# Whole expert blocks in paired slot halves, and layer two's filter taps in row pairs, in a two-layer hybrid encoder

## What is computed

```python
for i in range(DEPTH):                                   # DEPTH = 2
    h = modulate(rms_norm(x, norm1_g[i]), sh1, sc1)
    proj = h @ w_in[i]                                   # 1024 x 6656
    y_hy = hyena_mixer(...)      # its filters: k = (sin-MLP(z) @ w4) * decay
    y_at = dilated_attention_mixer(q, k, v)
    x = x + g1 * ((sigmoid(gate_hy) * (y_hy @ w_br_h[i]) + sigmoid(gate_at) * (y_at @ w_br_a[i])) @ w_out[i])
    h = modulate(rms_norm(x, norm2_g[i]), sh2, sc2)
    x = x + g2 * grouped_moe(h, router_w, router_bias, moe_w1[i], moe_w3[i], moe_w2[i])
return rms_norm(x, final_g)
# grouped_moe: two experts a token;  y += gate_e * ((silu(t @ w1[e]) * (t @ w3[e])) @ w2[e])
```

## Time and profile before

| | us |
|---|---|
| median of 3 runs | 1050.93 (1049.51 to 1054.65) |
| the profiled execution | 1051.37 |
| its span | 1049.6 |
| PE busy | 1001.3 (95%) |
| DVE busy | 564.4 (54%) |
| ACT busy | 188.5 (18%) |
| POOL busy | 40.0 (4%) |
| read from memory | 329.47 MB |

### The profile page before, as it was taken

How to read it: one execution, slowest core, us unless ns; L and a number is a source line. 1 busy time by engine, 2 the same in 40 slices (tenths; PEclk the granted TensorE clock), 3 DMA queues, 4 the chain that set the end, 5 groups by cost and what they waited for, 6 DMA issues and landing times.

```text
span 1049.6 us, 18343 instructions
## 1 busy us (share of the span) xinstructions
PE 1001.3 (95%) x7711; PEld 603.9 (58%) x7711; DVE 564.4 (54%) x1192; ACT 188.5 (18%) x395; POOL 40.0 (4%) x82
## 2 busy tenths in 40 slices
PE   6999999999999999999999999999999999999784
PEld 3688667667785444443358866765878534444321
DVE  4578795868786223352235779672758622333112
ACT  4031001211233121011131110132123311110102
POOL 2100100010000000000010010001000000000000
PEclk9999999999999999999999999999999999999997
DMA  9998946297976999999999894627875599999991
GB/s 310 385 383 299 309 162 242 71 315 287 407 300 219 421 387 420 421 420 421 421 397 367 287 328 163 222 71 273 312 277 213 199 421 421 421 419 421 421 419 76
DMA packets 91851, 333.88 MB, mean 318 GB/s; under 512 B 5724, under 2 KB 6027, under 8 KB 66933
## 3 DMA queue, kind: packets, MB, share of 16 engines
q1 hardware_dynamic: 87937, 323.56, 79.4%
q0 software_dynamic: 2944, 7.12, 2.3%
q10 hardware_dynamic: 884, 1.97, 0.6%
HBM read 329.47 MB, written 1.05 MB: 315 GB/s over the span
## 4 chain that ended last, share of the span: by engine, by line
PE 83%; DVE 9%; DMA 3%; issue 2%; ACT 1%; SPq 1%; DVEq 0%; ACTq 0%
PE bank L822 80%; DMA ring<-in_moe_w_dram 2%; SPq L721 1%; PE bank L1335 1%; PE bank L1111 1%; DVE wide L2004 0%; DVE area L2000 0%; DVE wide L1796 0%; PE bank L1164 0%; DVE x L2220 0%; PE bank L885 0%; DVE area L2219 0%; DVE area L2196 0%; DVE wide L2005 0%; DVE area L2003 0%
## 5 line engine op out<-in xcount | busy, mean ns | idle before, releaser
L822 PE MATMUL bank<-ring,hT 128*32 128x512 f32 (+3 forms) x1808 | 280.2, 548 | 4.9 <-DMA ring<-in_moe_w_dram 2.1
L822 PE MATMUL bank<-hT,ring 128*32 128x256 f32 (+1 forms) x2112 | 213.5, 381 | 0.7 <-DVE hT L1820 0.7
L822 PEld LDWEIGHTS bank<-ring,hT 128*32 128x32 f32 (+2 forms) x1808 | 119.8, 133 | 137.8 <-issue 132.5
L822 PEld LDWEIGHTS bank<-hT,ring 128*32 128x32 f32 (+1 forms) x2112 | 158.6, 132 | 53.3 <-issue 6.1
L822 PE MATMUL bank<-ring,area 128*32 128x512 f32 (+1 forms) x744 | 119.4, 571 | 0.9 <-ACT area L1670 0.9
L822 PE MATMUL bank<-area 32*64 32x64 f32 (+5 forms) x648 | 89.1, 363 | 0.0
L1796 DVE SCALAR_TENSOR_TENSOR area<-ring,wide,area 128x512 f32<-128x512 f32 x114 | 85.3, 748 | 2.7
L2428 DVE TENSOR_TENSOR area<-bank,area 128x512 f32<-128x512 f32 x14 | 9.7, 692 | 128.9 <-PE bank L822 128.9
L822 PE MATMUL bank<-wide,hT 128*32 128x512 f32 (+1 forms) x376 | 76.8, 584 | 1.4 <-DMA ring<-in_moe_w_dram 1.4
L822 PEld LDWEIGHTS bank<-ring,area 128*32 128x32 f32 (+1 forms) x744 | 43.8, 121 | 55.2 <-issue 50.1
L822 PEld LDWEIGHTS bank<-area 32*64 32x64 f32 (+4 forms) x648 | 37.9, 145 | 45.6 <-issue 44.4
(11 more groups left out here) (302 smaller groups left out, 1082.1 us busy)
## 6 DMA issues: line engine op xcount, KB each, us to landing
ring<-in_moe_w_dram SPq DMA_DIRECT2D x136, 1024.0 KB, 15.2
ring<-in_w_ada_dram SPq DMA_DIRECT2D x24, 2048.0 KB, 14.5
ring<-in_w_in_dram SPq DMA_DIRECT2D x24, 2048.0 KB, 12.3
wide<-in_moe_w_dram SPq DMA_DIRECT2D x32, 1024.0 KB, 12.9
cst<-in_moe_w_dram SPq DMA_DIRECT2D x13, 1024.0 KB, 13.2
area<-in_moe_w_dram SPq DMA_DIRECT2D x11, 1024.0 KB, 13.7
ring<-in_w_out_dram SPq DMA_DIRECT2D x4, 2048.0 KB, 8.6
ring<-in_w_br_h_dram SPq DMA_DIRECT2D x4, 1536.0 KB, 6.7
```

What stands on the lines that cost most here:

```text
L822: return pe.matmul(dst, lhsT, rhs, start=start, stop=stop, skip_group_check=True)
```

## The change

It has two parts, in one kernel.

**Whole blocks.** `place_blocks` now looks, at the first half of a block of steps 1 to 5, among the oldest two free slots for one whose other half stands at most one place behind it or before it in the list. If there is one, the two halves of that expert's matrix go together into this pair, as one DMA of 2 MiB ([128, 4096], 16 KiB a partition instead of 8), which SP issues where the first half stood; it waits for the release of both slots, and both halves of the matrix are ready when all 2 MiB have landed. In layer one 20 blocks are loaded whole, in layer two 23; every other one is as before. What is behind moves to other slots and so waits for other releases.

**Taps in pairs.** The w4 pieces of b = 0 stay on rows 64 to 127, those of b = 1 now land on rows 0 to 63, and GpSimd copies layer two's rows of `fh` also to rows 0 to 63 (one DMA more, 64 x 257). The products are issued by turns from the upper and the lower rows, into banks 2 to 5. Step 3 does 4 of them, before `up(3, 1)`, with no wait for DVE between them; the other 4 are done in step 4, before `up(4, 1)`. DVE reads them there too, so in step 4 ahead of `butterfly`. `scatter` waits for DVE bank by bank.

```diff
@@ place_blocks
-                    u, old = free.pop(0)
-                    while (L, u) in LAST and b[0] > LAST[L, u]:
+                    if (L, b) in whole and half:
+                        continue
+                    free = [f for f in free if b[0] <= LAST.get((L, f[0]), STEPS)]
+                    near = [i for i in range(2) if free[i][0] < TABLE and free[i][0] ^ 1 in [f[0] for f in free[:i + 2]]]
+                    if half == 0 and b[0] in WHOLE_STEPS and near:
+                        u = free[near[0]][0] & ~1
+                        olds = [old for f, old in free if f in (u, u + 1)]
+                        free = [f for f in free if f[0] & ~1 != u]
+                        whole.add((L, b))
+                        for h in range(2):
+                            part = (L, kind, b, h)
+                            plan[part] = halves[u + h], u, landings[u] + 16, olds[:1] if olds[0] == olds[1] else olds
+                            free.append((u + h, part))
+                    else:
                         u, old = free.pop(0)
-                    plan[key] = halves[u], u, landings[u] + 16, [old]
-                    free.append((u, key))
+                        plan[key] = halves[u], u, landings[u] + 16, [old]
+                        free.append((u, key))
...
@@ taps_in, tap, tap_bank
-        def taps_in(L, s, spot):
-            return range(4 * spot, 4 * spot + 4) if L + 1 < DEPTH and s == TAPS_STEP else ()
+        def taps_in(L, s):
+            first = 4 * (s - TAPS_STEP)
+            return range(first, first + 4) if L + 1 < DEPTH and s in (TAPS_STEP, TAPS_STEP + 1) else ()
+
+        def tap(l, i):
+            return i % 2 * 4 + i // 2 if l else i
+
+        def tap_bank(l, i):
+            return bank[2 + i % 4] if l else filter_bank(l, i % 2)
...
@@ SP
+                    if (L, b) in whole:
+                        dst, part = pairs[u // 2], slice(0, 2 * rows)
...
@@ GpSimd
+                    pool.wait_ge(p_kt, 8)
+                    pool.dma_start(fh[0:FFN, :], fh[FFN:2 * FFN, :]).then_inc(s_taps, 16)
...
@@ taps, on PE
-                    if u >= 2:
-                        pe.wait_ge(v_kt, l * 12 + u - 1)
+                    if l == 0 and i >= 2:
+                        pe.wait_ge(v_kt, i - 1)
+                    elif l and i >= 4:
+                        pe.wait_ge(v_kt, l * 12 + i - 3)
...
-                    mm(dst, fh[l * FFN:(l + 1) * FFN, first:first + P], hw4(l, b, n), True, True).then_inc(p_kt, 1)
+                    mm(tap_bank(l, i)[:, 0:HW2], fh[tap_rows(l, b), first:first + P], hw4(l, b, n), True, True)\
+                        .then_inc(p_kt, 1)
...
@@ scatter
-                            if L + 1 < DEPTH and k == 2 and s + 1 in (TAPS_STEP, TAPS_STEP + 1):
-                                pe.wait_ge(v_kt, (L + 1) * 12 + 4 * (s + 2 - TAPS_STEP))
+                            if taps_in(L, s + 1):
+                                pe.wait_ge(v_kt, (L + 1) * 12 + 4 * (s + 1 - TAPS_STEP) + k + 1)
...
@@ DVE, step s
-                    for u in taps_in(L, s, 0):
-                        decayed(u, L + 1)
+                    for i in taps_in(L, s):
+                        decayed(i, L + 1)
                     if L + 1 < DEPTH and s == TAPS_STEP + 1:
                         butterfly(L + 1, 0)
```

More of the change, by code:

```diff
@@ L78 @@
 TABLE, TAIL, ROWS = EXTRA + 4, EXTRA + 5, EXTRA + 6
+WHOLE_STEPS = range(1, 6)
 LAST = {(0, EXTRA): 3, (0, EXTRA + 1): 3, (0, EXTRA + 2): 1, (0, EXTRA + 3): 1, (1, EXTRA + 2): 3, (1, EXTRA + 3): 3}
@@ L224, in trunk_kernel @@
         halves += [cst[:, C_IC:C_IC + 4 * W]]
+        pairs = ring + [wide[:, h * 8 * W:(h + 1) * 8 * W] for h in range(2)]
         Kr = hy[:, 0:2 * HY].rearrange("p (m c) -> p m c", m=2)
@@ L370, in trunk_kernel, with tap_rows @@
         fing = g1b
+        def tap_rows(l, b):
+            half = l - b if l else 0
+            return slice(half * FFN, (half + 1) * FFN)
         def hw4(l, b, n):
-            rows = slice(l * FFN, (l + 1) * FFN)
+            rows = tap_rows(l, b)
             if l == 0:
                 return taps0[rows, b * HY + n * HW2:b * HY + (n + 1) * HW2]
-            if (b, n) == (1, 1):
-                return hT[rows, 0:HW2 // P, P:SEQ]
-            return ((rates, vec_rows), (attended,))[b][n][rows, 0:HW2]
+            return ((rates, vec_rows), (attended, vec_rows))[b][n][rows, 0:HW2]
         bank = [ctx.enter_context(nc.psum_tensor(f"bank{i}", [P, 512], F32)) for i in range(8)]
@@ L552, in trunk_kernel @@
         plan = {}
+        whole = set()
         def place_blocks():
@@ L683, in _ @@
             for L, kind, b, half in loads:
+                if half and (L, b) in whole:
+                    continue
                 _, u, _, olds = plan[L, kind, b, half]
@@ L719, in _ @@
                     name, order = ("moe_w1", "moe_w3", "moe_w2")[m], "(p k) f -> p k f"
-                    part = slice(half * (NF if m == 2 else ND) // 2, (half + 1) * (NF if m == 2 else ND) // 2)
+                    rows = (NF if m == 2 else ND) // 2
+                    part = slice(half * rows, (half + 1) * rows)
+                    if (L, b) in whole:
+                        dst, part = pairs[u // 2], slice(0, 2 * rows)
                     sp.dma_start(dst.rearrange("p (k f) -> p k f", f=D if m == 2 else FE),
@@ L809, in _ @@
                             src = t["hf_w4"][1, :, b * HY + n * HW2:b * HY + (n + 1) * HW2]
-                            if (b, n) == (1, 1):
-                                src = src.rearrange("k (a f) -> k a f", f=P)
                             pool.dma_start(hw4(1, b, n), src).then_inc(s_taps, 16)
+                    pool.wait_ge(p_kt, 8)
+                    pool.dma_start(fh[0:FFN, :], fh[FFN:2 * FFN, :]).then_inc(s_taps, 16)
             pool.wait_ge(p_up, DEPTH * STEPS * 2)
@@ L1384, in next_filter @@
                         rates_to_all(L + 1)
-                    if taps_in(L, s, spot) or spectra_in(L, s, spot):
+                    here = taps_in(L, s) if spot == 0 else ()
+                    if here or spectra_in(L, s, spot):
                         pe.wait_ge(v_acc, (L * STEPS + s - 1 + spot) * 4)
-                    for u in taps_in(L, s, spot):
-                        taps(u, L + 1)
+                    for i in here:
+                        taps(i, L + 1)
                     for u in spectra_in(L, s, spot):
@@ L1854, in shift_and_scale, with decayed @@
                     dv.wait_ge(v_A1, l + 2)
-                def decayed(u, l):
+                def decayed(i, l):
+                    u = tap(l, i)
                     b, lt, n = u // (2 * NT), u // 2 % NT, u % 2
                     dv.wait_ge(a_dec, 8 * l + u + 1)
-                    dv.wait_ge(p_kt, l * 8 + u + 1)
+                    dv.wait_ge(p_kt, l * 8 + i + 1)
                     taps = decays[l][:, b, lt, n * HW2:(n + 1) * HW2]
-                    dv.tensor_tensor(taps, filter_bank(l, n)[:, 0:HW2], taps, ALU.mult).then_inc(v_kt, 1)
+                    dv.tensor_tensor(taps, tap_bank(l, i)[:, 0:HW2], taps, ALU.mult).then_inc(v_kt, 1)
                 def butterfly(l, half):
@@ L2433, in _ @@
                         rows_to_h().then_inc(v_hg, 1)
-                    for u in taps_in(L, s, 1):
-                        decayed(u, L + 1)
                     for h in range(2):
```

10 lines of the change are left out of this document (4 added, 6 removed).

## The result

| | kernel before | the change |
|---|---|---|
| first comparison: median, us | 1050.93 (1049.51 to 1054.65, 7 runs) | 1057.04 (1054.71 to 1060.52, 7 runs) |
| ratio | | 1.0049 [1.0029, 1.0070] |
| both once more, in a later comparison | 1052.71 | 1059.8, ratio 1.0076 [1.0051, 1.0101] |
| span of the profiled execution, us | 1049.6 | 1058.6 |

The account below looks back on a forecast made before the run. The prediction took the weight stream on SP's queue to bound both mixtures, with PE waiting on landings. Layer one's later `up(5, 1)` +3.8, slow clock +1.7, layer two -0.4 made +5.1 us: 1056.0 us, range 1050 to 1061.

Parts of the forecast that it names:

- The stream bounds the middle of layer one: Layer one, `up(5, 1)`: weights only 4.0 us ahead of PE, so anything PE saves earlier beyond that is waited away.
- Granularity: Layer one, first half of `up(5, 1)`: with whole blocks it needs MiB 78 instead of MiB 75.
- The slow clock behind the wait: Layer one, after PE idles 8 us before `up(5, 1)`: products run at about half clock, adding 1.7 us.
- The restart, 3.4 us: Layer one: first load waits for both halves of `up(0, 0)`, so the stream starts 3.4 us late.
- The gap at MiB 49: Layer one: new gap, whole w2 block (MiB 49 and 50) waits for slots freed by `down(2)`; about 1.0 us.
- The count itself: Landing times from queue start, 2.494 us a MiB, gaps, and 5.2 us for start and last landing; held within 0.1 us.
- Packet size, 0.09 us a block: Whole blocks with 16 KiB packets take 0.09 us less than two halves; 1.6 us for 18 blocks in layer one.
- The rival of slower packets: 16 KiB packets slower than two of 8 KiB, 5.1 us a block: 10.4 us with the clock, 1061.3 us; 15%.
- slices under 415 GB/s: Sign that the forecast is wrong: slices over 428 or under 415 GB/s.
- Taps, 1.3 us for four: Four tap products, paired side by side, take 1.3 us; 2.6 if the pairs don't overlap.
- The wait before `up(4, 1)`, 1.5 us: Layer one: PE comes at 449.3 us, MiB 62 of the whole w3 blocks at 450.8, so 1.5 us waited.
- Layer two, -0.4 us: Wait moves to `down(5)`, which needs MiB 84 instead of 81; then PE runs without a wait, ending 0.4 us earlier.

Follow-up runs that it names:

- the change again: The change run once more, unaltered, on the chip of the later kernels; ratio to the kernel before 1.0076 [1.0051, 1.0101].
- taps_only: The change's taps with every block loaded in halves as in the kernel before; 1054.45 us beside 1053.94, ratio 1.0016.
- one_block: The change's taps, only the three w3 blocks of layer one's step 5 whole, all others in halves; 1057.01 us beside 1053.14, ratio 1.0042.
- grain: The change, but with the three w3 blocks of layer one's step 5 loaded in halves; 1055.69 us, ratio 1.0018.
- same_rows: The change with the tap products in plain order, so only one of three neighbouring pairs has different rows; single run, 1056.88 us.
- restart: The change, but the w3 block of layer one's step 1, expert 1, where the queue starts again, loaded in halves; 1059.28 us, ratio 1.0070.
- whole_only: The change's whole blocks in both layers, with the taps as in the kernel before; 1060.43 us beside 1053.94, ratio 1.0069.
- keep_clock: The change with 16 dummy 128x256 products ahead of `up(5, 1)` in layer one, in the wait; 1058.81 us, ratio 1.0063.
- four_split: The change with the restart's block, MiB 25 and 26, MiB 49 and 50, and step 5's w3 of layer one in halves; 1053.1 us beside 1052.71, ratio 1.0005.
- l2_whole: The change's taps, layer one's blocks all in halves, layer two's 23 whole as in the change; 1053.34 us beside 1053.14, ratio 1.0007.

## Why the prediction was right, and where it wasn't

The total was right, +5.1 us predicted and 5.2 between the profiles counted from S (6.8 with the change again; 6.1 and 7.1 between medians), and so was its place. That `up(5, 1)` started within 0.1 us of the forecast was partly luck: two errors in the count cancel. Step by step:

- **The stream bounds the middle of layer one; what PE saves there is waited away.** Right. taps_only shows it by itself: 5.1 us earlier at `up(5, 1)`, 0.2 us at the end of the layer.
- **Granularity: `up(5, 1)` needs MiB 78 in place of 75.** Right, and the main term: one_block makes 4.3 us of it alone, grain takes 3.2 away.
- **The slow clock behind the wait, 1.7 us.** Right in kind; the size is 1.6, 1.6 (same_rows), 2.0, 2.2, 2.6, 2.7 and 2.7 us in the seven profiles that wait with all of `up(5, 1)` and no filler. The one row of before that gave 1.7 was at the low end of a spread.
- **The restart, 3.4 us, as a term of the sum.** The step that failed. The restart is 3.4 us late, and yet undoing it gains nothing. Already at MiB 21 the landings are only 2.3 us late: it is issued at 333.92 us before and at 338.29 in the change, and lands 9.7 and 11.5 us later, at S + 17.2 and S + 19.5. I added the 3.4 us to the stream's lateness and then looked for gaps only where the kernel before had one and at MiB 49. The gap at MiB 25, whose first half had needed no release that was still to come, was missed; it takes back most of what an early start gains (MiB 26 lands at S + 32.3 in restart and 33.1 in the change again), and the gaps behind it the rest (MiB 53 at S + 100.9 and 101.0). The lateness, seen as bytes, is in the change's two profiles 0.6 to 0.8 MiB by S + 90, 1.6 to 2.0 us, and 0.4 to 0.6 MiB by S + 160. With the gaps counted out, mine was 3.4 - 2.4 + 1.0 = 2.0 at S + 90, less 0.8 for the nine whole blocks up to there: near the right size, from the wrong parts. The gap at MiB 49 showed near S + 86, as windows of 2 us at 295 to 377 GB/s, in restart, grain, whole_only, keep_clock, same_rows and the change again, and not in the change's first profile.
- **The count itself.** For halves it gives MiB 78 at 330.12 + 61 x 2.494 + 2.4 + 5.2 = 489.85, S + 163.4; the four profiles with halves before it have it at S + 161.5 to 161.8. The 5.2 us of start and last landing were taken over from layer two, and are about 3.5 in layer one. So the slack was not 4.0 but 5.8 us: in the kernel before MiB 75, issued at 461.84, lands 18.8 us later, at S + 154.2, and PE comes at S + 160.0. The lateness of the whole blocks at `up(5, 1)` was not 0.35 us, as the sum had it, but 0.9 to 1.9 by the landings of the change's two profiles. These two errors cancel in S + 163.8 (seen: 163.7, 162.8, 163.7 with same_rows).
- **Packet size, 0.09 us a block.** Right within what can be told: 0.08 to 0.16 by q1's share of two pages, and 0.1 by the landings, since from MiB 53 to MiB 78 the kernels with halves take 62.2 to 62.4 us, and those with 8 whole blocks in between 61.5 to 61.6. The rival of slower packets is out. Of its signs one did appear, slices under 415 GB/s: 402 from 344 to 370 us, which holds the gap at MiB 25, and 413 from 873 to 900 us. The three cycles a packet that the Trainium skill gives ("DMA: Bandwidth & Descriptors", Why small descriptors are slow), an estimate of 0.03, are too few for these rows; by them the sum would have been 1.1 us higher in layer one and 1.3 in layer two, 2.4 and not 1.3. The 2.0 us a DMA that the prediction took from the same page of the Trainium skill (Anatomy of one DMA) are given there for DMAs that GpSimd issues; q1 is SP's, and its loads stand behind each other.
- **Taps, 1.3 us for four.** 1.56 seen, 2.84 with most neighbours on the same rows; the two bounds were 1.3 and 2.6. The stretch of slow clock behind the second group of before is gone, as counted.
- **The wait before `up(4, 1)`, 1.5 us.** 1.13 seen.
- **Layer two, -0.4 us.** -0.1 in the first profile, +1.4 with the change again; the waits stand where they were said to. What the prediction had not priced is a slow clock behind the wait for `down(5)`, 1.7 us in two of ten profiles. A term of 0.4 us can't be judged by single profiles.

Still open is why single landings ahead of MiB 53 come late while the bytes don't show it: whole_only and the change again had moved the same by S + 160 (60.7 and 60.8 MiB), and MiB 78 is there at S + 165.1 and 162.8. The layout alone doesn't say it: the change itself moves by 1 us from one execution to another.

## What to carry to other kernels

Where an engine waits for the first part of a load, find the k-th byte that releases it before and after the loads are merged: 3 MiB later in a stream of 2.49 us a MiB weighed more here than all that fewer and larger DMAs brought (about 0.1 us a block). A merged load waits for the later of two releases, and the queue can run dry there, as at MiB 25; a start that is made earlier is only worth what the next such gap leaves of it, so count all gaps, not the first. And before speeding up an engine ahead of a stream, look whether the same stream also ends the stage: then the saving is waited away twice.

## What the runs showed of the hardware

- The granted clock of PE fell to half behind waits of 3.64 to 7.6 us in layer one (grain, four_split, and all that wait with whole w3 blocks there), but not behind 3.20 and 3.26 us (l2_whole, taps_only). In layer two the length of the wait doesn't tell: `up(5, 1)`'s second half ran slowly behind 3.80 us in the change (5.34 us) and behind 2.56 us in l2_whole (5.31), and at full speed behind 3.80 us in same_rows (32 products in 3.64 us). At 1.2 in place of 2.4 GHz the work behind one wait lost between 1.6 and 2.9 us (2.9 in layer two of four_split, 6.58 us for 32 products).
- Early in the program the granted clock between 23 and 40 us differs from execution to execution (1.00 down to 0.70) with the same instructions, and moves everything behind it by up to 5.6 us. That is as much as the effect under study; only marks counted from a later event compare two profiles to 1 us.
- Two 128x384 float32 products over 64 rows each, on the lower and the upper rows in turn and into different banks, ran 1.8 times as fast as with two of three neighbouring pairs on the same rows (1.56 and 2.84 us for four).
- Between 385 and 530 us, where about half the bytes came in runs of 16 KiB, the queue moved 423 GB/s, with 8 KiB alone 421.
